# Normalising two softmaxes by a product with a diagonal tile of inverse row sums, in place of a scaling on VectorE and a transpose

## What is computed

```python
s = jnp.where(key_pos[None, :] <= q_pos[:, None], s, -jnp.inf)      # MLA
p = jax.nn.softmax(s, axis=-1).astype(v.dtype)
return jnp.einsum('bhqk,bkhv->bqhv', p, v)

logits = jnp.where((dist >= 0)[:, None], logits, -jnp.inf)          # DSA
p = jax.nn.softmax(logits, axis=-1).astype(c_sel.dtype)
return jnp.einsum("bhqk,bqkc->bqhc", p, c_sel)
```

## Time and profile before

| | before |
|---|---|
| median of three executions | 2856.41 us |
| the profiled execution | 2849.98 us |
| its span in the trace | 2848.2 us |
| PE busy, share of the span | 93% |
| PE weight loads | 73% |
| DVE | 51% |
| ACT | 23% |
| POOL | 40% |
| mean granted clock of PE, of full speed | 0.962 |

### The profile page before, as it was taken

How to read it: one execution, slowest core, us unless ns; L and a number is a source line. 1 busy time by engine, 2 the same in 40 slices (tenths; PEclk the granted TensorE clock), 3 DMA queues, 4 the chain that set the end, 5 groups by cost and what they waited for, 6 DMA issues and landing times.

```text
span 2848.2 us, 30951 instructions
## 1 busy us (share of the span) xinstructions
PE 2662.3 (93%) x11724; PEld 2070.7 (73%) x11724; DVE 1448.1 (51%) x1985; ACT 663.1 (23%) x1297; POOL 1142.3 (40%) x764
## 2 busy tenths in 40 slices
PE   8999899999999999999999999999888778899998
PEld 6888688888666578888876777766555546688886
DVE  4754574565544435546566744544334447555521
ACT  2004420111233312102132133322213232222200
POOL 4333355555312145555544533322222113455554
PEclk9999999999899999999999999999888879999999
DMA  6433465656312156565644744434433214465565
GB/s 200 125 115 123 129 192 194 193 194 195 122 60 76 43 167 190 194 195 189 210 156 152 229 148 154 157 126 133 159 123 117 96 45 140 146 195 194 191 195 168
DMA packets 148857, 436.62 MB, mean 153 GB/s; under 512 B 13872, under 2 KB 18160, under 8 KB 148720
## 3 DMA queue, kind: packets, MB, share of 16 engines
q1 hardware_dynamic: 64224, 200.29, 23.9%
q0 software_dynamic: 67584, 201.35, 20.2%
q10 hardware_dynamic: 16912, 33.14, 3.2%
HBM read 417.90 MB, written 16.83 MB: 153 GB/s over the span
## 4 chain that ended last, share of the span: by engine, by line
issue 38%; PE 32%; POOL 23%; DVE 3%; DMA 2%; ACT 2%; DVEq 1%; ACTq 0%; POOLq 0%; SPq 0%
POOL w_lo L450 18%; PE bank L502 9%; PE bank L504 8%; PE bank L505 8%; POOL w_hi L432 5%; PE bank L703 1%; DMA projections<-spill_out 1%; PE bank L1117 1%; PE bank L777 0%; PE bank L780 0%; PE bank L779 0%; DMA residual<-x_in 0%; PE bank L1077 0%; DVE next_gained L2234 0%; PE bank L1107 0%
## 5 line engine op out<-in xcount | busy, mean ns | idle before, releaser
L450 POOL TENSOR_TENSOR w_lo<-w_raw,w_hi 128x1024 fp32r<-128x1024 f32 x376 | 908.9, 2418 | 15.1 <-DMA w_hi<-stream 7.1
L432 POOL DMA_DIRECT2D w_hi<-stream x376 | 227.2, 604 | 1673.1 <-PE bank L502 1505.4
L502 PE MATMUL bank<-x_hi,w_hi 128*128 128x512 f32 x1472 | 590.5, 401 | 26.8 <-POOL w_lo L450 13.5
L504 PE MATMUL bank<-x_lo,w_hi 128*128 128x512 f32 x1472 | 578.6, 393 | 0.0
L505 PE MATMUL bank<-x_hi,w_lo 128*128 128x512 f32 x1472 | 578.0, 393 | 0.0
L502 PEld LDWEIGHTS bank<-x_hi,w_hi 128*128 128x128 f32 x1472 | 279.8, 190 | 96.9 <-issue 20.9
L505 PEld LDWEIGHTS bank<-x_hi,w_lo 128*128 128x128 f32 x1472 | 279.6, 190 | 59.7
L504 PEld LDWEIGHTS bank<-x_lo,w_hi 128*128 128x128 f32 x1472 | 279.9, 190 | 57.5 <-issue 2.4
L1983 DVE TENSOR_TENSOR relu_sq<-relu 128x512 f32<-128x512 f32 x64 | 179.1, 2799 | 94.6 <-ACT relu L1395 94.6
L502 PE MATMUL bank<-hidden_hi,w_hi 128*128 128x512 f32 x512 | 199.2, 389 | 0.0
L504 PE MATMUL bank<-hidden_lo,w_hi 128*128 128x512 f32 x512 | 199.2, 389 | 0.0
(11 more groups left out here) (435 smaller groups left out, 4450.8 us busy)
## 6 DMA issues: line engine op xcount, KB each, us to landing
w_hi<-stream POOLq DMA_DIRECT2D x376, 512.0 KB, 4.8
w_raw<-stream SPq DMA_DIRECT2D x376, 512.0 KB, 3.7
projections<-spill_out ACTq DMA_DIRECT2D x56, 256.0 KB, 2.0
ssm_x<-projections ACTq DMA_DIRECT2D x4, 1024.0 KB, 7.2
gate_tiles<-projections ACTq DMA_DIRECT2D x16, 256.0 KB, 3.2
ssm_z<-projections ACTq DMA_DIRECT2D x4, 1024.0 KB, 9.5
residual<-x_in SPq DMA_DIRECT2D x4, 512.0 KB, 10.7
toeplitz_hi<-toeplitz_rows_hi POOLq DMA_DIRECT2D x4, 512.0 KB, 6.5
```

The source lines that it names most:

```text
L432: e.dma_start(in_slot(whi, t % SLOTS, o), in_stream(o)).then_inc(hi_ready[t % SLOTS], 16)
L450: e.tensor_tensor(wlo[:, s, :], raw[:, s, :], whi[:, s, :].bitcast(F32), ALU.subtract).then_inc(lo_ready, 1)
L502: mm = e.matmul(out, wh, rh, start=first, stop=False)
L504: e.matmul(out, wh, rl, start=False, stop=False)
```

## The change

The scaling of the exponentials goes. In its place DVE multiplies the 128 x 128 identity by the inverse row sums of the item, one for each partition, into a diagonal tile (`mdiag` in MLA, `ddiag` in DSA, rings of three). PE then uses the unscaled exponentials as the stationary operand and the diagonal tile as the moving one of an ordinary fp32 matmul, where before it had a transpose with the identity. The product is the transpose with each column scaled, which is the same tile as before. Waits and signals stay as they were.

```diff
+        mdiag, ddiag = at("mla_inverse_sums", 126, [P, 3, P]), at("dsa_inverse_sums", 106, [P, 3, P])
@@ TensorE, MLA (DSA the same with ddiag)
                         for k in range(m % 4 + 1):
-                            mm = e.transpose(bank[3 + m % 2][:, chunk(k)], mpr[:, m % 3, chunk(k)], ident)
+                            mm = e.matmul(bank[3 + m % 2][:, chunk(k)], mpr[:, m % 3, chunk(k)], mdiag[:, m % 3, :],
+                                          start=True, stop=True)
                         mm.then_inc(at_t, 1)
@@ VectorE, MLA (DSA the same with ddiag)
-                        w = (m % 4 + 1) * P
                         e.wait_ge(at_e, m + 1)
                         e.reciprocal(mri[:, m:m + 1], mrs[:, m:m + 1])
                         e.drain()
-                        ts(mpr[:, m % 3, 0:w], mpr[:, m % 3, 0:w], mri[:, m:m + 1], None, ALU.mult).then_inc(at_p, 1)
+                        ts(mdiag[:, m % 3, :], ident, mri[:, m:m + 1], None, ALU.mult).then_inc(at_p, 1)
```

More of the change, by code:

```diff
@@ L1131, in sparse_attention @@
                         for k in range(m % 4 + 1):
-                            mm = e.transpose(bank[3 + m % 2][:, chunk(k)], mpr[:, m % 3, chunk(k)], ident)
+                            mm = e.matmul(bank[3 + m % 2][:, chunk(k)], mpr[:, m % 3, chunk(k)], ddiag[:, m % 3, :],
+                                          start=True, stop=True)
                         mm.then_inc(at_t, 1)
@@ L2288, in sparse_attention @@
                     if 0 <= m < D_ITEMS:
-                        wd = (m % 4 + 1) * P
                         e.wait_ge(at_e, n0 + m + 1)
@@ L2292, in sparse_attention @@
                         e.drain()
-                        ts(mpr[:, m % 3, 0:wd], mpr[:, m % 3, 0:wd], mri[:, m:m + 1], None, ALU.mult).then_inc(at_p, 1)
+                        ts(ddiag[:, m % 3, :], ident, mri[:, m:m + 1], None, ALU.mult).then_inc(at_p, 1)
                     for x in D_STEPS[n]:
```

## The result

| | before | after |
|---|---|---|
| median of the executions | 2856.2 us (4) | 2879.49 us (4, from 2877.54 to 2880.12) |
| the profiled execution | 2849.98 us | 2880.12 us |
| its span | 2848.2 us | 2878.3 us |

The changed kernel is slower: 1.0079 times the time before, with a 95% interval from 1.0062 to 1.0097, so by 18 to 28 us. The forecast was 2886 us with a range from 2873 to 2899. The profiled executions differ by 30.1 us, the medians by 23.3.

The account below looks back on a forecast made before the run. PE was taken to bound both attentions; 33.6 us for chunks plus 2.1 for low clock less 6.0 swallowed gave +29.7 us, which on the median of 2856.41 us made 2886 us, range 2873 to 2899.

Parts of the forecast that it names:

- PE bounds both stretches: MLA and DSA: PE, busy 226.31 of 231 and 364.49 of 396 us, bounds both; added PE work lengthens them.
- The price of a chunk: Both attentions: each fp32 matmul replacing a transpose adds 0.105 us at full clock, 33.6 us for 320 chunks.
- Rival 2, the dear matmul: The first chunk of each of 128 items costs 0.32 us: +12.8 us, 2899 us; chance 9%.
- A factor of four: PE's 320 chunks: by the skill, a matmul costs four transposes, 0.46 us, 110 us in all, about 2966 us; not adopted.
- What the waits swallow: PE's waits in MLA and DSA: hidden PE work and DVE's narrower instruction give a credit of 6.0 us.
- The low clock: Low-clock parts of MLA and DSA: 20 chunks cost a further 0.105 us each, 2.1 us.
- The sum: Whole kernel: 33.6 + 2.1 - 6.0 = +29.7 us on the profiled execution of 2849.98 us, 2879.7 us.
- The median: Whole kernel: the same addition on the median of 2856.41 us gives the forecast, 2886 us.
- Rival 1, the clock comes back: Low-clock stretch at MLA's start: ordinary matmuls raise the clock at once, up to 7.0 us back, 2879 us; chance 11%.
- Rivals 3 and 4: 3: DVE chain in DSA the true bound, 2844 us, chance 2%; 4: product as cheap as transpose, 2854 us, 3%.

Follow-up runs that it names:

- the halves: Two kernels, against the kernel before: the change in MLA alone, 2867.57 us, 1.0060 times before; the change in DSA alone, 2866.68 us, 1.0053 times before.

## Why the prediction held

- **PE bounds both stretches.** Right. Its idle time was 4.7 and 31.9 us, and nothing but PE's own work grew. By the halves, MLA's growth is there without DSA's change and the other way round.
- **The price of a chunk.** The step was right, its size too low. I took 0.22 - 0.115 = 0.105 us, 33.6 us in all. It was 0.12, 38.5 us: PE is busy for 19.6 + 17.5 = 37.1 us more. Most of the gap is in my subtraction: 0.22 is a product in the middle of a run, 0.115 the mean of four transposes with their dearer start. In rows 4 both stand in a run, 0.22 and 0.11, and that difference is 35.2 us. The rest is the start of a group, some 2 us more for products than for transposes.
- **Rival 2, the dear matmul.** Fell as a term of 12.8 us. Some first products did take 0.32 us, but others 0.22 or 0.27, and transposes start dearer too: what the start adds is some 2 us in all.
- **A factor of four.** The Trainium skill, "TensorE: Matmul & The Clock Gate", terminology table, has the transpose mode four times as fast for fp32, which would have given about 2966 us. The starts show 0.24 to 0.115 us, a factor of two.
- **What the waits swallow.** Right in kind, too small. I gave 6.0 us in all; 3.0 + 4.4 + 1.6 = 9.0 us went from the three rows of waits, and idle time fell by 2.8 + 7.1 = 9.9. Of it 2.6 us are VectorE's narrower instruction (I said 2.0), 6.4 us are PE's work inside waits (I said 4.0). By the kernel with matmuls by the identity, the ten waits of DSA swallowed 2.8 where I said 2.5; the miss is in MLA, 2.0 for 0.7, and in the copy, 1.6 for 0.8.
- **The low clock.** 2.1 us was meant for 20 chunks, ten in each attention. In MLA ten chunks were at the low level, in DSA seven. Four chunks took 1.81 us there (791.75 to 793.56), against 0.87 for four transposes, so 0.235 more each and not 0.21. That gives about 2 us, the forecast's size.
- **The sum.** +29.7 us was forecast, 27.3 is what the two attentions grew by in the profiled executions, and 30.1 the two whole executions. Two errors cancelled: PE's busy time grew by 37.1 us where 33.6 + 2.1 = 35.7 were forecast, and idle time fell by 9.9 where 6.0 were. That 29.7 meets the 30.1 so closely is luck on top, since 2.8 of the 30.1 arose ahead of MLA, in a low stretch that is there with transposes too, and DSA happened to have 3.4 us less at the low level than before.
- **The median.** This is the largest miss, 6.5 us. I added the difference of profiles to the median of before. The executions of before spread from 2848 to 2861 us over all runs, and the profiled one had been near the bottom; those of the kernel after lie within 3 us. The difference of medians is 23.3. The granted clock goes the same way: 0.960 or 0.961 in the four executions of after, 0.958 or 0.959 in the median of before on each of three chips. That isn't shown to come from the products, since the kernel with matmuls by the identity ran at 0.954 to 0.957 in three executions of four.
- **Rival 1, the clock comes back.** Fell, though its 2879 us is the number that was measured; that is chance. The first steps of MLA, now with ordinary matmuls, are at 0.50 from 777 to 795 us with PE busy for all of it, and MLA has 20.5 us at the low level in both kernels. That also speaks against the rule of the Trainium skill, "TensorE: Matmul & The Clock Gate", Part 4, as the cause of this stretch: without a single transpose in the loop the clock stayed low as long. Over all profiles this first low stretch lasts 17.1 to 23.9 us with fp32 transposes and 17.1 to 20.5 with fp32 products.
- **Rivals 3 and 4.** Fell: narrower scalings by themselves are worth 2.6 us, and the records and the time between starts both doubled.

## What to carry to other kernels

A transpose by the identity and a product by a diagonal tile look alike, but in fp32 the second costs two records for one and 0.24 us for 0.115, on the engine that bounds the kernel, to save 0.1 to 0.2 us an item on one that is idle for half of the time. Compare prices by the distance between starts, and compare like with like: both in the middle of a run, or both with the start of the group, which can be dearer. Work added ahead of a wait is free up to the wait's length, so sum the waits before you charge it; and the wait is worth more than the swap: moving the convolution one step back on VectorE gave 11 us by the medians without touching PE. Before two profiles of one stretch are compared, compare how long each was at the low clock.

## What the runs showed of the hardware that was not expected

- In fp32r, the product by the diagonal tile took 0.125 us a chunk, nearly a transpose's 0.115, yet the granted clock of MLA was 0.93 in that profile. With fp32 transposes it was 0.94 to 0.96 over the profiles, with fp32 products 0.95 to 0.97. The ten executions in fp32r ran at 0.952 to 0.959, those of before on that chip, but for one at 0.914, at 0.956 to 0.961. I can't say from these runs which property of the work did it, or whether the format did.
- An instruction of VectorE in DSA that overlaps POOL's subtraction can last until just after that ends: in the kernel after several of 128 columns took 2.96 us, where the mean in MLA is 0.287. Narrowing the instruction to 128 columns did not make this rarer, 20 of 64 against 17.
- The low stretch at the start of MLA is there in every profile. It follows a wait of 1.6 us and lasts through some 17 to 24 us of work with no idle time; the same MLA code took 234.06 us in the kernel before and 237.47 us, at 0.94, in the kernel with VectorE's units one step later. Differences of 3 us in a stretch of this kernel are therefore no evidence of anything else, unless the low stretches are as long in both.
